# Dilated attention: the transpositions two rounds behind the scores in the same two buffers, and output chunks begun over six of their eight tiles

## What is computed

```
q = (h @ w_q).reshape(bsz, seq, B_GROUPS, B_HEADS, B_HEAD_DIM)
q = _rms(q, q_gain[:, None, :]) * (B_HEAD_DIM ** -0.5)
...
    s = jnp.einsum('birhd,bjrhd->bhrij', qb, kb).astype(f32) + biases[g][None, :, None]
    s = jnp.where(valid[None, None], s, -jnp.inf)
    lse = jax.nn.logsumexp(s, axis=-1)
    p = jnp.exp(s - lse[..., None]).astype(vb.dtype)
    o = jnp.einsum('bhrij,bjrhd->birhd', p, vb)
...
wts = jax.nn.softmax(jnp.stack(lses), axis=0)
o = jnp.einsum('gbqh,gbqhd->bqhd', wts, jnp.stack(outs))
return o @ w_o
```

## Time and profile before

| | us |
|---|---|
| median of 3 runs (2180.75 to 2193.05) | 2185.96 |
| the profiled execution | 2191.01 |
| its span | 2189.2 |
| PE busy in the span | 2011.5 |
| first scores of the block, start | 1796.69 |
| end of its four output chunks | 1987.5 |

### The profile page before, as it was taken

One profiled execution on the slowest core, in us unless ns is written; L12 is line 12 of the kernel. 1 busy time (PEld: TensorE's weight loads), 2 busy tenths in 40 slices (PEclk: granted clock), 3 DMA queues, 4 the chain that ended last, 5 costly groups with the idle time before them and its releaser, 6 DMA issues.

```text
span 2189.2 us, 36847 instructions
## 1 busy us (share of the span) xinstructions
PE 2011.5 (92%) x15863; PEld 1925.3 (88%) x15863; DVE 1163.3 (53%) x1356; ACT 991.6 (45%) x1157; POOL 506.5 (23%) x142
## 2 busy tenths in 40 slices
PE   7887999989999989999887999999999988869999
PEld 6875899988899979999886999999899977649998
DVE  5336577665577764337784643433444355536443
ACT  4325444355443453336334443476643455625433
POOL 1100122322022221320340123333222312121322
PEclk9867999999899999999998999999999999979999
DMA  7300345443245525555321455445455554314552
GB/s 261 136 18 1 116 155 195 166 162 135 97 144 198 194 98 192 172 182 183 125 79 56 156 189 176 160 163 169 152 182 189 177 166 141 105 61 148 179 186 102
DMA packets 57314, 321.13 MB, mean 147 GB/s; under 512 B 5694, under 2 KB 19125, under 8 KB 19829
## 3 DMA queue, kind: packets, MB, share of 16 engines
q1 hardware_dynamic: 55444, 313.93, 41.5%
q10 hardware_dynamic: 1760, 5.63, 0.7%
HBM read 318.41 MB, written 1.12 MB: 146 GB/s over the span
## 4 chain that ended last, share of the span: by engine, by line
PE 72%; DVE 12%; issue 7%; ACT 5%; POOL 2%; DMA 2%; SPq 0%; ACTq 0%; DVEq 0%; POOLq 0%
PE bank L371 22%; PE bank L372 21%; PE bank L373 21%; DVE lo L344 3%; ACT hi L338 1%; PE bank L430 1%; DVE xl L839 1%; DVE arena L519 1%; PE bank L1512 1%; POOL lo L344 1%; ACT arena L1673 1%; DMA arena<-rel_rows 1%; POOL arena L501 1%; DVE arena L1587 1%; PE bank L1067 1%
## 5 line engine op out<-in xcount | busy, mean ns | idle before, releaser
L371 PE MATMUL bank<-xh,hi 128*128 128x256 f32 x3208 | 923.6, 288 | 37.1 <-DVE xl L839 20.2
L372 PE MATMUL bank<-xl,hi 128*128 128x256 f32 x3208 | 916.5, 286 | 0.0
L373 PE MATMUL bank<-xh,lo 128*128 128x256 f32 x3208 | 916.1, 286 | 0.0
L338 ACT ACTIVATE hi<-ring 128x2048 fp32r<-128x2048 f32 x291 | 550.5, 1899 | 476.6 <-PE bank L373 471.1
L344 POOL TENSOR_TENSOR lo<-ring,hi 128x2048 fp32r<-128x2048 f32 x90 | 421.1, 4680 | 1409.4 <-ACT hi L338 1409.4
L344 DVE TENSOR_TENSOR lo<-ring,hi 128x2048 fp32r<-128x2048 f32 x201 | 524.4, 2610 | 384.5 <-ACT hi L338 384.3
L371 PEld LDWEIGHTS bank<-xh,hi 128*128 128x128 f32 x3208 | 624.1, 195 | 49.9 <-issue 32.8
L372 PEld LDWEIGHTS bank<-xl,hi 128*128 128x128 f32 x3208 | 624.2, 195 | 0.6 <-issue 0.5
L373 PEld LDWEIGHTS bank<-xh,lo 128*128 128x128 f32 x3208 | 623.9, 194 | 0.2
L371 PE MATMUL bank<-gh,hi 128*128 128x256 f32 x1056 | 302.3, 286 | 16.7 <-DVE gl L775 15.9
L372 PE MATMUL bank<-gl,hi 128*128 128x256 f32 x1056 | 301.1, 285 | 0.0
(11 more groups left out here) (263 smaller groups left out, 1857.6 us busy)
## 6 DMA issues: line engine op xcount, KB each, us to landing
ring<-in_ffn_in SPq DMA_DIRECT2D x132, 1024.0 KB, 4.9
ring<-in_ffn_out SPq DMA_DIRECT2D x66, 1024.0 KB, 4.9
ring<-in_kv SPq DMA_DIRECT2D x24, 1024.0 KB, 4.8
ring<-in_hg_in SPq DMA_DIRECT2D x16, 1024.0 KB, 4.9
ring<-in_od_in SPq DMA_DIRECT2D x12, 1024.0 KB, 5.0
ring<-in_dq SPq DMA_DIRECT2D x12, 1024.0 KB, 4.9
ring<-in_ev_in SPq DMA_DIRECT2D x11, 1024.0 KB, 4.9
arena<-rel_rows SPq DMA_DIRECT2D x16, 384.0 KB, 5.6
```

What stands on the lines that cost most here:

```text
L338: nc.scalar.activation(hi[n % RING][:, 0:words[n]], ring[n % RING][:, 0:words[n]], ACT.Copy).then_inc(hi_ok, 1)
L371: nc.tensor.matmul(out_, lh, rh, start=start, stop=False, **kw)
L372: nc.tensor.matmul(out_, lh, rl, start=False, stop=False, **kw)
L373: return nc.tensor.matmul(out_, ll, rh, start=False, stop=stop, **kw)
```

## The change

Five edits, all in `Soft` under a flag `woven` that this block alone sets, or in the block itself:

1. The lag is two rounds. In round i PE issues S(i,g), then (for g = 2) the chunk in `step`, then T(i-2,g), in all rounds. There are ten rounds instead of nine. The buffers stay two, so the mask of part g of unit i waits for T(i-2,g), part by part, where before it waited once for the whole unit.
2. DVE's reciprocal for unit i-1 (and with it POOL's scaling) comes between the masks and the maxima of unit i. ACT copies T(i-2,0) and T(i-2,1), then takes the exponentials of unit i, then copies T(i-2,2) in the rounds that have a chunk inside.
3. The take-out of chunk 4 moves behind the masks of unit 0, the squares of chunk 4 behind its exponentials; P(5) waits for the take-out of chunk 3 only.
4. The bias transfers of units 1, 2, 3 and 4 are issued after chunk loads 9, 10, 12 and 13 instead of 10, 11, 13 and 14.
5. Output chunks 12 and 13 are multiplied over tiles 0 to 5 at the end of round 8, and half of chunk 14 over tiles 0 to 2 and 3 to 5 inside round 9; the rest follows. The four output chunks go to banks 0 to 3 instead of 4 to 7.

```diff
-                    if i >= s.lag and i not in s.exps_first:
+                    if i >= s.lag and (i not in s.exps_first or s.woven):
                         turn(i - s.lag, g)
-                if i >= s.lag and i in s.exps_first:
+                if i >= s.lag and i in s.exps_first and not s.woven:
                     for g in range(ns):
                         turn(i - s.lag, g)
...
-                if i >= s.nr:
+                if i >= s.nr and not s.woven:
                     dve.wait_ge(*s.at("turned", 2 * ns * (i - s.nr + 1)))
...
                     dve.wait_ge(*s.at("qk", w + 1))
+                    if i >= s.nr and s.woven:
+                        dve.wait_ge(*s.at("turned", 2 * (w - s.nr * ns) + 2))
                     for e in range(2):
                         nc.vector.tensor_tensor(a[e][:, g, :], soft_bank(w, e)[:, 0:384], un["subs"][e][g]["add"],
                                                 ALU.add).then_inc(soft_sem["masked"], 1)
+                if s.woven and i >= 1:
+                    weights(i - 1)
                 for e in range(2):
                     dve.wait_ge(*s.at("masked", 2 * ns * (i + 1) - 1 + e))
                     nm = s.nm[:, 2 * (i % 4) + e, :]
...
-                if not s.by_pool:
+                if not s.woven:
...
-                if s.late and i >= 1:
+                if s.late and i >= 1 and (not s.woven or i == U):
                     weights(i - 1)
...
+                if s.woven:
+
+                    early = ns - 1 if i in s.filled else ns
+                    if j >= 0:
+                        turned(j, range(early))
+                    if i < U:
+                        exps(i)
+                    if j >= 0:
+                        turned(j, range(early, ns))
+                    s.hook(s.mid, "act", i, act)
+                    if j >= 1:
+                        pair_out(j - 1)
+                    s.hook(s.after, "act", i, act)
+                    continue
...
+        def pe_part_of(pe, n, B, h, ks, tiles):
+
+            if h == 0 and 0 in ks:
+                wait_split(pe, n)
+                nc.tensor.matmul(B[:, :], zero16[:, :], zero16[:, :].unsqueeze(1).broadcast_to([1, 4, P]), start=True,
+                                 stop=False, skip_group_check=True)
+            wh, wl = slot(n, CW, hi), slot(n, CW, lo)
+            e = slice(h * P, (h + 1) * P)
+            for k in ks:
+                tiles(k)
+                last = product(B[:, h * T:(h + 1) * T], wh[:, k, e], wl[:, k, e], xh[:, k, :], xl[:, k, :],
+                               False, k == KT - 1, skip_group_check=True)
+            if h == 1 and KT - 1 in ks:
+                last.then_inc(chunk_mul, 1)
 
...
+
+            return bank[i if before.get(b) == "dilated" else 4 + i]
...
-            soft = Soft(units, 3, False, att, pt, NM, RR, copies, [DK[:, p, :] for p in range(N_HELD)], True)
+            soft = Soft(units, 3, True, att, pt, NM, RR, copies, [DK[:, p, :] for p in range(N_HELD)], True)
...
-                    pe.wait_ge(*soft.at("pt", 12 * (hg - 1)))
+                    pe.wait_ge(*soft.at("pt", 12 * (hg - 1) - 6))
...
-                        pe.wait_ge(lin, c)
+                        pe.wait_ge(lin, c if c > 5 else 4)
...
-                return {4: [0], 10: [1], 11: [2], 13: [3], 14: [4], 15: [5, 6, 7]}.get(c, [])
+                return {4: [0], 9: [1], 10: [2], 12: [3], 13: [4], 15: [5, 6, 7]}.get(c, [])
...
+                    if i == 0:
+                        take_out(dve, 4)
                     if i in inside:
                         take_out(dve, inside[i])
...
-            soft.turn_after = {j: (log_ok, 3 * hg + 3) for j, hg in normed.items()}
-            soft.step = {(i, 2): lambda pe, c=c: project(pe, c) for i, c in inside.items()}
+            def out_ready(pe):
+
+                return lambda k: pe.wait_ge(*soft.at("o", k + 1)) if k >= N_HELD else pe.wait_ge(held_l, 1)
+
+            def out_first(pe):
+
+                pe.wait_ge(*soft.at("masked", 48))
+                for c in (0, 1):
+                    for h in range(2):
+                        pe_part_of(pe, n0 + 12 + c, bank[c], h, range(6), out_ready(pe))
+
+            def out_third(ks):
+                def run(pe):
+                    pe_part_of(pe, n0 + 14, bank[2], 0, ks, out_ready(pe))
+                return run
+
+            def out_rest(pe):
+                for k in (6, 7):
+                    for c in (0, 1):
+                        for h in range(2):
+                            pe_part_of(pe, n0 + 12 + c, bank[c], h, (k,), out_ready(pe))
+                pe_part_of(pe, n0 + 14, bank[2], 0, (6, 7), out_ready(pe))
+                pe_part_of(pe, n0 + 14, bank[2], 1, range(8), out_ready(pe))
+                pe_half(pe, n0 + 15, bank[3], "fm", 0)
+                pe_half(pe, n0 + 15, bank[3], "fm", 1)
+
+
+            soft.turn_after = {max(j - 1, 0): (log_ok, 3 * hg + 3) for j, hg in normed.items()}
+            soft.filled = set(inside)
+            soft.step = ({(i, 2): lambda pe, c=c: project(pe, c) for i, c in inside.items()}
+                         | {(9, 1): out_third(range(3)), (9, 2): out_third(range(3, 6))})
             soft.after["pe"] = ({i: lambda pe, c=c: project(pe, c) for i, c in behind.items()}
-                                | {i: lambda pe, hg=hg: means(pe, hg) for i, hg in normed.items()})
+                                | {i: lambda pe, hg=hg: means(pe, hg) for i, hg in normed.items()} | {8: out_first})
             soft.mid["dve"] = {i: dve_mid(i) for i in range(6)}
             soft.after["dve"] = {i: lambda dve, c=c: take_out(dve, c) for i, c in behind.items()}
...
             soft.mid["act"] = {i: lambda act, c=c: squares(act, c) for i, c in inside.items()}
+            soft.mid["act"][0] = lambda act: (squares(act, 4), squares(act, 5))
...
                                  | {i: lambda act, hg=hg: roots(act, hg) for i, hg in normed.items()})
...
             def pe_part(pe):
                 project(pe, 0)
```

More of the change, by code:

```diff
@@ L381, in build, with __init__ @@
         class Soft:
-            def __init__(self, units, ns, late, att, pt, nm, rr, copies, held=(), by_pool=False):
-                self.by_pool = by_pool
+            def __init__(self, units, ns, late, att, pt, nm, rr, copies, held=(), woven=False):
+                self.woven = woven
                 self.units, self.ns, self.late, self.att, self.pt, self.nm, self.rr = units, ns, late, att, pt, nm, rr
@@ L387, in __init__ @@
                 self.nr = len(att)
+                self.filled = set()
                 self.before = {"pe": {}, "dve": {}, "act": {}}
@@ L583, in pair_out, with exps @@
                     nc.scalar.activation(h, src, ACT.Copy).then_inc(soft_sem["oh"], 1)
-            def exps(u):
-                for e in range(2):
+            def exps(u, heads=(0, 1)):
+                for e in heads:
                     act.wait_ge(*s.at("max", 2 * u + e + 1))
@@ L591, in exps, with turned @@
                                          accum_out=rr[:, 0:1]).then_inc(soft_sem["exp"], 1)
-            def turned(j):
-                for g in range(ns):
+            def turned(j, parts=None):
+                for g in range(ns) if parts is None else parts:
                     w = j * ns + g
@@ L847, in dve_prep @@
                     dve.wait_ge(y_bank if kind == "y" else chunk_mul, val)
-                    y = bank[4 + i][:, :].rearrange("p (e t) -> p e t", e=2)
+                    y = y_bank_of(b, i)[:, :].rearrange("p (e t) -> p e t", e=2)
                     if scale is None:
@@ L908, in dve_rs, with y_bank_of @@
             dve.wait_ge(rs_new, st)
+        def y_bank_of(b, i):
+            return bank[i if before.get(b) == "dilated" else 4 + i]
         def outputs_in_xh(r):
@@ L2052, in make_dilated @@
             soft.before["act"] = {6: held_high}
-            soft.exps_first = set(inside)
             def pe_part(pe):
@@ L2064, in pe_part @@
                 soft_pe(pe, soft)
-                pe_residual(pe, "dilated", n0 + 12,
-                            lambda k: pe.wait_ge(*soft.at("o", k + 1)) if k >= N_HELD else pe.wait_ge(held_l, 1))
+                out_rest(pe)
             def dve_part(dve):
@@ L2073, in dve_part @@
                 norms(dve, 0)
-                take_out(dve, 4)
                 soft_dve(dve, soft)
@@ L2082, in act_part @@
                 roots(act, 0)
-                for c in (3, 4):
-                    squares(act, c)
+                squares(act, 3)
                 soft_act(act, soft)
```

## The result

The changed kernel takes 2207.23 us (median of 4 runs, 2204.65 to 2209.84); the kernel before took 2187.89 in the 4 runs beside it. The ratio is 1.0091, 95% interval [1.0058, 1.0124]: slower, by an amount that a measurement can tell. The forecast was 2204, in the range 2189 to 2213.

What follows compares the result with a forecast made beforehand. PE is busy 92% overall; in the block it waits for POOL's scaling (19.5 us), with DVE waiting for bias transfers (19.1). -4.2 + 8.0 + 9.7 + 8.0 - 3.6 = +17.9 us on 2186 gives 2204, range 2189 to 2213.

Steps and rivals of the forecast that it cites:

- rounds 0 and 1: First two rounds: unit 0's T and V leave (-4.8), on balance +0.6 from waits; 46.1 becomes 41.9 us.
- S(5,0) to the end of the chunks: Last rounds and output chunks: 87.3 becomes 83.7 us, -3.6, though carrying a whole unit of T and V more.
- DVE's chain in rounds 2 to 4: The last mask waits for T(i-2,2) behind the chunk, so DVE's queued work is uncovered: +8.0, +9.7, +8.0 us.
- The rival "faster": DVE's chain stays covered, rounds 2 to 4 grow under 3 us together: -14, 2172 us; chance 0.09.
- Two terms of the chain: DVE operations before take-outs in rounds 1 to 4: low half priced at 2.4 us, norms at 2.1.
- P(7)'s wait: Round 1: P(7), without T(0,.) in front, waits 2.9 us for the take-out of chunk 6.
- the rival "slower still": P(7), P(9) and P(11) also start at low clock, 8.9 us each for 5.9: +27, 2213 us; chance 0.14.
- The means at the low clock: Means after a long PE idle time take 5.4 us, an estimate between 2.8 and about twice that.
- The rival "same time": Means take 2.8 us even after idling and PE keeps 2.4 GHz in rounds 7 and 8: +6, 2192; chance 0.19.
- The estimate of 4.7 by the Trainium skill: A unit's bias transfers by the skill's fit, against the profile's 8.9 us; the sum would be +14.
- cover POOL's unit 7: After round 8's T and V, 72 matmuls of chunks 12 and 13 (8.7 us) cover POOL's work on unit 7.
- signs named: PE idle 6 to 8 us in rounds 2 to 4, S(5,0) about 21 us later, chunks' end about 18, POOL waits gone.

Runs made afterwards that it cites:

- turn_before_chunk: Kernel after, with T(i-2,2) ahead of the query chunk on PE in rounds 2 to 4: ratio to before 1.0018, block 192.8 us.
- pool_behind_chain: Kernel after, with POOL's scaling of units 0 to 3 held until DVE has taken out the round's query chunk: block 204.7 us, 6.0 less.
- bias_by_part: Kernel after, with the bias transfers of units 6 and 7 issued part by part, each with its own semaphore: block 206.8 us, 4.0 less.
- edit5_undone: Kernel after, with the output products of rounds 8 and 9 moved back behind the last T and V: block 208.4 us, 2.3 less.
- fill_lag_one: Kernel before, with 24 output products ahead of T(6,0) and 66 at the start of round 8: 2176.05 us, ratio 0.9943, block 174.5 us.

## Why the prediction was right

The times are from S to S, as in the forecast.

| piece | before | forecast | after |
|---|---|---|---|
| rounds 0 and 1 | 46.1 | 41.9 | 44.0 |
| round 2 | 17.9 | 25.9 | 25.6 |
| round 3 | 21.5 | 31.2 | 32.2 |
| round 4 | 17.9 | 25.9 | 25.7 |
| S(5,0) to the end of the chunks | 87.3 | 83.7 | 83.3 |
| change of the block | | +17.9 | +19.9 |

**DVE's chain in rounds 2 to 4** was right in place, in cause and nearly in size. The forecast's idle times were 6.8 us and some 8; they are 7.63 and 9.47. turn_before_chunk shows the cause. The rival "faster", by which the chain stays covered, had its condition at less than 3 us in these rounds; they grew by 26.1. One reading in the forecast is off without consequence: before, the last mask of unit 2 was not done before P(8), but ran in its first microsecond.

**Two terms of the chain were too small.** The low half was taken at 2.4 and took 3.22 in rounds 2 and 4, the norms at 2.1 and took 3.52 in rounds 1 and 3. Both lie beside POOL's scaling, which edit 2 put there, and pool_behind_chain shows that they fall back without it. In the totals of rounds 2 and 4 this does not show, since the estimate for the means was too large by 1.0 to 1.1. A duration that the profile of before shows alone was used for a place where the change sets another engine's work beside it.

**P(7)'s wait** was taken at 2.9 and is 4.28, from the same norms. P(7) then took 8.2 us (1826.18 to S(2,0) at 1834.42), where I had it at full clock, 5.9: the mechanism of the rival "slower still", in one of its three places; P(9) and P(11) stayed at 5.9. The wait and the slower P(7) are +3.7; the means took back 0.8 and the rest of my walk was 0.8 too long, which leaves +2.1. The change was to win 4.2 us in these rounds and won 2.1.

**The means at the low clock**, an estimate of 5.4, took 4.7, 4.3 and 4.5 in this execution (in others up to 5.5); that took back 0.7 to 1.1 us in each of three places. The rival "same time" rested on 2.8, which no mean had after an idle time of 6.7 us or more.

**Rounds 5 to 9.** From S(5,0) the masks of unit 6 ended after 24.8 us (forecast 24.7; here two errors cancel by luck: the norms took 3.51 beside POOL for 2.1, and the held output 0.68 for 2.0, which before had lain beside POOL), those of unit 7 after 42.2 (42.6), the last V of unit 6 after 52.8 (54.2), and the end took 30.4 (29.5). The bias transfers went from issue at 1942.73 to the mask at 1951.69 in 9.0 us; the row of 8.9 was the right price, and bias_by_part shows that this wait counts. The estimate of 4.7 by the Trainium skill (DMA: Bandwidth & Descriptors, Anatomy of one DMA), whose fit is per transfer and for the gpsimd path, did not hold for these four that SP issues: it would have made round 7 some 4 us shorter. One step was wrong without moving the sum: the 72 products were to "cover POOL's unit 7", but POOL was done before them, and edit5_undone shows that the products of rounds 8 and 9 cost 1.6 us.

**Sum.** Against the forecast the five pieces are off by +2.1, -0.3, +1.0, -0.2 and -0.5 us: +19.9 for +17.9. That the total came so near is in part luck, since terms that were too small (norms, low halves, P(7)) met terms that were too large (the means, the held output, round 8). The median rose by 19.3 against the runs beside it. Of the signs named, the idle times, what ended them, the mask right behind T(.,2) and the missing wait before T(7,0) are there, and the longest wait for POOL is 2.8 us. S(5,0) and the end of the chunks came 17.7 and 13.6 us later than before, not 21 and 18, because the block began 6.3 us earlier; counted from S(0,0) they are 24.0 and 19.9 later.

## What to carry to other kernels

Before an item is moved behind a long matmul run, list what is queued on the other engines behind the item that waits for it: there the long run was the cover, and it is now the wait. Filling work has no worth of its own, only that of the wait it stands in; 72 products gained some 7 us at one lag, and at the other they and 18 more lost 1.6, so measure each edit in the kernel where it will stand. A wait that is closed by reordering two queues comes back one round later unless work is found to lie beside it.

## What the runs showed of the hardware

- DVE and POOL slow each other in some operations on float32 in SBUF. Norms (three of 128 x 512) took 3.52 us beside POOL and 2.07 without it, a low half (128 x 2048) 3.22 to 3.47 and 2.28; POOL's four operations took 4.91 beside norms, 6.51 beside a low half and 4.46 alone. Both DVE operations read two tiles in SBUF. The maxima, which read one, kept their 0.95 and 0.54 us beside POOL in round 2.
- The rows read like turns, not like a shared speed. In round 2 of the kernel after, the low half (1851.19 to 1854.41) begins while POOL is in its third operation; that one keeps its 1.47 us, the low half is 0.94 longer, and POOL's fourth takes 2.87 where it takes 0.82 alone. In round 6 of the kernel before, DVE begins 0.05 us ahead of POOL; the low half keeps its 2.29, and POOL's first operation takes 3.57 for 1.47:

```profile
1850.80 1.47 POOL L505 TENSOR_TENSOR arena<-arena 128x768 f32<-128x768 f32 x1
1852.23 2.87 POOL L505 TENSOR_TENSOR arena<-arena 128x384 f32<-128x384 f32 x1
```

```profile
1914.38 2.29 DVE L344 TENSOR_TENSOR lo<-ring,hi 128x2048 fp32r<-128x2048 f32 x1
1914.43 3.57 POOL L501 TENSOR_TENSOR arena<-arena 128x768 f32<-128x768 f32 x1 [16.69 <-DVE arena L537]
```

- After 4.28 us without work, PE ran at the low of its two clock levels (1.2 GHz; products 0.21 us apart for 0.12); after waits of 1.45 and 1.71 the means took 2.84, as at 2.4. Between them it was mixed: after 2.09 to 3.53 us a chunk took 7.3 to 7.4, where it takes 5.9 dense. S(7,1) took 1.65 for 0.92 after a wait of 2.59; two of 1.86 and 1.66 stood shortly ahead of it. In the kernel before S(0,1) took 1.61 after 3.58. The fall can also come later than the wait: in fill_lag_one S(1,1) ran at full clock after 3.73 us, and S(1,2), after 0.66, at the low one:

```profile
1813.19 0.92 PE L430 MATMUL bank<-arena 64*128 64x256 f32 x8 [3.73 <-DVE arena L519]
1814.77 1.65 PE L430 MATMUL bank<-arena 64*128 64x256 f32 x8 [0.66 <-DVE arena L519]
```

- The means behind waits of 6.4 to 7.6 us took 4.2 to 5.5 us, so the price of a restart varied by more than 1 us between executions.
